# The last two down rounds of each feed-forward, one token half after the other

## The reference, cut to what matters

```python
D_MODEL, SEQ, DEPTH, D_FF = 1024, 512, 2, 2816
def swiglu(h, w_in, w_out):
    g, u = jnp.split(h @ w_in, 2, axis=-1)
    return (jax.nn.silu(g) * u) @ w_out
# per layer i, m = nine modulation vectors from silu(c) @ w_mod[i] + b_mod[i]
h = h + 0.5 * m[2] * swiglu(modulate(rms_norm(h), m[0], m[1]), w_ff_in[i, 0], w_ff_out[i, 0])
a = modulate(rms_norm(h), m[3], m[4])
h = h + m[5] * mixer(a)          # Fourier mixing (i = 0) or convolution (i = 1)
h = h + 0.5 * m[8] * swiglu(modulate(rms_norm(h), m[6], m[7]), w_ff_in[i, 1], w_ff_out[i, 1])
```

## Time and profile before

| | us |
|---|---|
| median of 3 runs | 1851.25 (1850.66 to 1855.26) |
| span of the profiled execution | 1854.0 |
| TensorE busy in it | 1803.4 (97%) |
| VectorE busy in it | 1198.1 (65%) |
| ScalarE busy in it | 619.6 (33%) |
| mean granted TensorE clock | 0.989 |

### The profile page before, as it was taken

The page is one execution under the profiler, slowest core; times in us unless marked ns, Lnnn a source line. Parts: engine busy times, 40 slices in busy tenths (PEclk is TensorE's granted clock), DMA queues, the critical chain, the costliest instruction groups (busy, mean ns, idle before and its releaser), DMA issues.

```text
span 1854.0 us, 22066 instructions
## 1 busy us (share of the span) xinstructions
PE 1803.4 (97%) x8604; PEld 1486.5 (80%) x8604; DVE 1198.1 (65%) x1541; ACT 619.6 (33%) x796; POOL 171.7 (9%) x148
## 2 busy tenths in 40 slices
PE   5899999998999999999999999999999999999999
PEld 2688888888898888888988888889764898888888
DVE  5876767667867676666676766547798555444454
ACT  2522222234342223222432222225776542222221
POOL 0000000002110000000200000002995200000000
PEclk8999999998999999999999999999999999999999
DMA  7753634431436354363154353411120321313201
GB/s 279 273 201 114 212 127 155 185 113 47 136 114 227 114 176 164 122 218 114 69 196 145 140 200 113 136 68 46 46 91 25 116 88 69 136 68 113 90 23 69
DMA packets 160395, 238.10 MB, mean 128 GB/s; under 512 B 3805, under 2 KB 110509, under 8 KB 160204
## 3 DMA queue, kind: packets, MB, share of 16 engines
q1 hardware_dynamic: 160016, 236.99, 36.5%
q10 hardware_dynamic: 316, 0.23, 0.0%
HBM read 235.11 MB, written 2.10 MB: 128 GB/s over the span
## 4 chain that ended last, share of the span: by engine, by line
PE 84%; DVE 6%; POOL 4%; ACT 3%; DMA 1%; issue 1%; SPq 0%; POOLq 0%; DVEq 0%; ACTq 0%
PE bank L1670 15%; PE bank L1672 15%; PE bank L1677 15%; PE bank L1545 10%; PE bank L1547 10%; PE bank L1546 10%; POOL tmp_c L628 3%; DVE mod_acc L1025 2%; PE bank L1927 1%; DVE w_lo L992 1%; PE bank L1617 1%; PE bank L1615 1%; PE bank L1619 1%; DMA raw_pair<-in_w_mod 1%; POOL sq_sum L593 1%
## 5 line engine op out<-in xcount | busy, mean ns | idle before, releaser
L1670 PE MATMUL bank<-a_hi,w_hi 128*128 128x512 f32 x1408 | 551.9, 392 | 6.2 <-ACT a_hi L686 4.7
L1672 PE MATMUL bank<-a_hi,w_lo 128*128 128x512 f32 x1408 | 548.9, 390 | 0.0
L1677 PE MATMUL bank<-a_lo,w_hi 128*128 128x512 f32 x1408 | 434.5, 390 | 1.3 <-DVE a_lo L1100 1.2
L1670 PEld LDWEIGHTS bank<-a_hi,w_hi 128*128 128x128 f32 x1408 | 265.0, 188 | 63.4 <-issue 6.3
L1218 DVE SCALAR_TENSOR_TENSOR h<-bank,half_gate,h 128x512 f32<-128x512 f32 x320 | 233.3, 745 | 121.7 <-PE bank L1547 121.1
L1677 PEld LDWEIGHTS bank<-a_lo,w_hi 128*128 128x128 f32 x1408 | 264.6, 188 | 57.3 <-DVE a_lo L1100 2.3
L1672 PEld LDWEIGHTS bank<-a_hi,w_lo 128*128 128x128 f32 x1408 | 264.9, 188 | 56.2 <-issue 1.4
L1545 PE MATMUL bank<-p_hi,w_hi 128*128 128x512 f32 (+1 forms) x768 | 289.5, 377 | 1.5 <-DVE h L1225 0.9
L1547 PE MATMUL bank<-p_lo,w_hi 128*128 128x512 f32 (+1 forms) x768 | 287.5, 374 | 0.0
L1546 PE MATMUL bank<-p_hi,w_lo 128*128 128x512 f32 (+1 forms) x768 | 287.4, 374 | 0.0
L992 DVE TENSOR_TENSOR w_lo<-raw_pair,w_hi 128x2048 fp32r<-128x2048 f32 x102 | 235.4, 2308 | 51.8 <-ACT w_hi L800 47.9
(11 more groups left out here) (197 smaller groups left out, 1849.2 us busy)
## 6 DMA issues: line engine op xcount, KB each, us to landing
raw_pair<-in_w_ff_in SPq DMA_DIRECT2D x88, 1024.0 KB, 7.0
raw_mod<-in_w_mod SPq DMA_DIRECT2D x66, 1024.0 KB, 8.4
raw_down<-in_w_ff_out SPq DMA_DIRECT2D x44, 1024.0 KB, 8.6
raw_pair<-in_conv_w_in SPq DMA_DIRECT2D x8, 1024.0 KB, 6.8
raw_pair<-in_w_mod SPq DMA_DIRECT2D x6, 1024.0 KB, 16.0
raw_pair<-in_fnet_w_out SPq DMA_DIRECT2D x4, 1024.0 KB, 6.1
raw_pair<-in_conv_w_out SPq DMA_DIRECT2D x4, 1024.0 KB, 6.7
raw_mod<-in_x SPq DMA_DIRECT2D x4, 512.0 KB, 5.6
```

Of the source, the lines that this page charges most:

```text
L1670: pe.matmul(ps[banks + s][:], tile_hi, a_hi[:, k], start=k == 0, stop=False, skip_group_check=True)
L1672: pe.matmul(ps[banks + s][:], tile_lo, a_hi[:, k], start=False, stop=False, skip_group_check=True)
L1677: ins = pe.matmul(ps[banks + s][:], w_hi[b][:, s * KD + k], a_lo[:, k], start=False, stop=k == KD - 1, skip_group_check=True)
```

## The change

Down round 9 is no longer done in the last step. Rounds 9 and 10 are done together after it, first for token half 0 and then for half 1. Both rounds of a chunk and half add up in one PSUM bank, and h is updated once for the two. Six banks (4, 5, 6, 7, 0, 1) are used in turn; since only six chunks fit, a half goes: round 9 d 0 to 5, round 10 d 0 and 1, round 9 d 6 and 7, round 10 d 2 to 7. Before the seventh chunk of round 9 TensorE waits for the update of the first. TensorE waits for `mod_row` of the last unit before the first of these products, in place of before the fourth chunk (d = 3) of the round. In the norm behind it, VectorE's `mod_columns` now stands ahead of the updates of half 0, the second weight unit is split later (ScalarE waits until round 9 has been read in both halves), VectorE's order is another, and `first_two` waits for the second unit only where it is first read. The transposes at the end of the kernel go through banks 2, 3, 0, 1, six of eight ahead of the last down chunk.

```diff
+    LAST_BANKS = [4, 5, 6, 7, 0, 1]
+    LAST_ROUNDS = [(NI - 2, range(6)), (NI - 1, range(2)), (NI - 2, range(6, KD)), (NI - 1, range(2, KD))]
     def last_round_h(f):
-        return HB[FF_PHASE[f]] + KD * (NI - 1)
+        return HB[FF_PHASE[f]] + KD * (NI - 2)
+        def last_bank(hf, d):
+            return ps[LAST_BANKS[(KD * hf + d) % len(LAST_BANKS)]][:, HALF[hf]]
...
 # ScalarE, ff_norm
-                act.wait_ge(s_take, last_round_h(f))
-                next_hi_unit()
                 for o in range(KD):
                     half_square(n, 0, o)
-                for o in range(3):
+                half_std(n, 0)
+                half_hi(n, 0, 0, layer, v)
+                half_hi(n, 0, 1, layer, v)
+                half_square(n, 1, 0)
+                act.wait_ge(s_down_read, f + 1)
+                next_hi_unit()
+                half_square(n, 1, 1)
+                half_hi(n, 0, 2, layer, v)
...
 # VectorE, ff_norm
+                mod_columns(call)
                 for d in range(KD):
                     flush_half(f, 0, d)
-                    if d == 3:
-                        next_lo_unit(0)
-                    if d == 6:
-                        next_lo_unit(1)
-                mod_columns(call)
-                for d in range(3):
-                    flush_half(f, 1, d)
                 half_rstd(n, 0)
-                flush_half(f, 1, 3)
-                for k in range(4):
+                for k in range(2):
                     half_normed(n, 0, k, layer, v)
-                    flush_half(f, 1, 4 + k)
+                    flush_half(f, 1, k)
+                for k in range(2):
+                    half_lo(n, 0, k, layer, v)
+                for k in range(2, 4):
+                    half_normed(n, 0, k, layer, v)
+                    flush_half(f, 1, k)
+                next_lo_unit(0)
+                flush_half(f, 1, 4)
+                next_lo_unit(1)
+                for k in range(2, 4):
+                    half_lo(n, 0, k, layer, v)
+                    flush_half(f, 1, 3 + k)
+                flush_half(f, 1, 7)
...
 # VectorE, ff_step
-                for d in range(KD):
-                    flush(f, i - 1, d)
                 if not last_step:
+                    for d in range(KD):
+                        flush(f, i - 1, d)
                     next_lo(f, i, 1, par)
...
 # TensorE
-                for b, use in units:
-                    pe.wait_ge(s_w[b], use + 1)
+                pe.wait_ge(s_w[units[0][0]], units[0][1] + 1)
...
-                    down(f, i - 1, 1 - par, unit)
+                    if not isinstance(i, int) or i < NI - 1:
+                        down(f, i - 1, 1 - par, unit)
+                    return unit
...
+                if unit is not None:
+                    pe.wait_ge(s_mod_row, unit + 1)
+            def last_down(f, r, hf, ds):
+                hs, final = HALF[hf], r == NI - 1
+                b, use = (DOWN_LAST[f][0], DOWN_LAST[f][1] + 1) if final else (DOWN[f][0], r + DOWN[f][1] + 1)
+                pe.wait_ge(s_w[b], use)
+                pe.wait_ge(s_p, 2 * NI * f + 2 * r + 2)
                 for d in ds:
+                    q, turn = KD * hf + d, len(LAST_BANKS)
+                    if not final and q < 4:
+                        pe.wait_ge(s_h, last_round_h(f) - 3 + d)
+                    elif not final and q < turn:
+                        pe.wait_ge(s_prod, 2 * NI * (f + 1) - 1)
+                    elif not final:
+                        pe.wait_ge(s_h, last_round_h(f) + q - turn + 1)
                     for j in range(2):
+                        ins = product(last_bank(hf, d), w_hi[b][:, j * KD + d], w_lo[b][:, j * KD + d],
+                                      p_hi[:, r % 2, j, hs], p_lo[:, r % 2, j, hs], not final and j == 0,
+                                      final and j == 1)
+                    if final:
+                        ins.then_inc(s_take, 1)
+                    elif q == 2 * KD - 1:
+                        ins.then_inc(s_down_read, 1)
+            def last_rounds(f, n):
+                for part, (r, ds) in enumerate(LAST_ROUNDS):
+                    last_down(f, r, 0, ds)
+                    if part == 1:
+                        mod_transpose(2 if f == 0 else 3 + f)
+                last_down(f, NI - 2, 1, range(3))
                 half_sums(n, 0)
+                last_down(f, NI - 2, 1, range(3, 6))
                 half_spread(n, 0)
+                for r, ds in LAST_ROUNDS[1:]:
+                    last_down(f, r, 1, ds)
+                pe.wait_ge(s_h, last_round_h(f) + KD + 4)
...
 # end of the kernel: OUT_BANK = [2, 3, 2, 3, 2, 3, 0, 1]
+            for r, ds in LAST_ROUNDS:
+                last_down(3, r, 0, ds)
+            last_down(3, NI - 2, 1, range(6))
+            out_transpose(0)
+            out_transpose(1)
+            last_down(3, NI - 1, 1, range(2))
+            last_down(3, NI - 2, 1, range(6, KD))
+            out_transpose(2)
+            out_transpose(3)
+            last_down(3, NI - 1, 1, range(2, 6))
+            out_transpose(4)
+            last_down(3, NI - 1, 1, range(6, 7))
+            out_transpose(5)
+            last_down(3, NI - 1, 1, range(7, KD))
+            out_transpose(6)
+            out_transpose(7)
```

More of the change, by code:

```diff
@@ L128, in hybrid_backbone @@
     PROJ = [(o, None) for o in range(KD - 2)] + [(o, hf) for hf in range(2) for o in (KD - 2, KD - 1)]
-    for prev, nxt, updates in ((FFA, FNET, KD * (NI + 1)), (FNET, FFB, len(PROJ)), (FFB, FFC, KD * (NI + 1)),
-                               (FFC, CONV, KD * (NI + 1)), (CONV, FFD, len(PROJ))):
+    for prev, nxt, updates in ((FFA, FNET, KD * NI), (FNET, FFB, len(PROJ)), (FFB, FFC, KD * NI),
+                               (FFC, CONV, KD * NI), (CONV, FFD, len(PROJ))):
         HB[nxt] = HB[prev] + updates
@@ L1224, in flush_half @@
                 dve.wait_ge(s_take, last_round_h(f) + KD * hf + d + 1)
[L1225 removed]
+                dve.scalar_tensor_tensor(out=h[:, d, hs], in0=last_bank(hf, d), scalar=half_gate[:, f, d:d + 1],
                                          in1=h[:, d, hs], op0=ALU.mult, op1=ALU.add).then_inc(s_h, 1)
@@ L1633, in first_two @@
                             for b, s, bank in tiles[:3]:
+                                if k == 0 and b == units[1][0]:
+                                    pe.wait_ge(s_w[b], units[1][1] + 1)
                                 half_product(b, s, bank, k, hs, False)
@@ L1761, in last_round @@
-            def last_round(f, n):
-                last_down(f, 0, range(4))
-                mod_transpose(2 if f == 0 else 3 + f)
-                last_down(f, 0, range(4, KD))
-                last_down(f, 1, range(4))
+                    unit = step(i, i % 2, f < 3 and i <= UNIT_STEPS[f])
+                if unit is not None:
[5 more added lines that the diff above has]
+                pe.wait_ge(s_p, 2 * NI * f + 2 * r + 2)
+                for d in ds:
+                    q, turn = KD * hf + d, len(LAST_BANKS)
[5 more added lines that the diff above has]
+                        pe.wait_ge(s_h, last_round_h(f) + q - turn + 1)
+                    for j in range(2):
+                        ins = product(last_bank(hf, d), w_hi[b][:, j * KD + d], w_lo[b][:, j * KD + d],
[5 more added lines that the diff above has]
+                        ins.then_inc(s_down_read, 1)
```

53 lines of the change are left out of this document (15 added, 38 removed).

## The result

The change makes the kernel slower. Its median is 1863.53 us of 4 runs (1862.91 to 1865.42) beside 1852.53 us of 4 runs of the kernel before (1850.66 to 1855.26): a ratio of 1.006 with a 95% interval of 1.0048 to 1.0073, +11.0 us by the medians. The forecast was 1860.5 us in a range of 1855.0 to 1865.0, slower by more than 0.3% with a chance of 0.76. The range holds the time; the forecast's own range, 1858 to 1863, does not, and the sum was 3.0 us short.

A forecast was written before the change was run, and what follows sets the result against it. TensorE, busy 97% of 1854.0 us, was taken as the bound. Ending terms of +4.4, +3.4, +0.2 and +1.3 made +9.3 us, added to 1851.25 (the span less 2.75): 1860.5 us, range 1855.0 to 1865.0.

The forecast's parts named there:

- The wait for `mod_row`: Ahead of the first down product in f = 0 and 1, TensorE waits 3.15 us each; before, this cost nothing.
- The clock behind it: After the `mod_row` wait, one half-rate stretch of 3.4 us, 1.6 us lost, in each of f = 0 and 1.
- The sign on the norm's stretches: The forecast is wrong if the norm's slow clock stretches, worth 6.2 us before, vanish.
- Rival A: Neither the idle 3.1 us nor the sums draw a half-rate stretch: +6.1 us, or +5 (1856.3); chance 0.20.
- Rival B: More or longer half-rate stretches behind the idle time or norm sums, +1.5 us each, 1864 with two or three; chance 0.20.
- Rival C: First wait under 1 us, clock up throughout: -0.2 us, or about -3 to -6 (1847); chance 0.05.
- Rival D: The Fourier stage's start hides part of f = 0's cost, leaving only 2 us: 1858; chance 0.55 together with the forecast.
- The later loads: SyncE loads the next weight pair some 12 us later, but it is needed over 40 us on: no cost.
- Half products and f = 3: Half products +0.6 us an ending; f = 3's last product 2 us later, tail 0.7 us shorter: +1.3 us.
- The squares of half 0: In the norm, TensorE waits 0.7 us for GpSimd's adds of 1.08 us each; 0.97 us before.
- The second weight unit: Split later, with VectorE parts of 1.6 us, it makes TensorE wait 1.15 us at the next stage.
- The sums of half 1: The sums behind three k of the next stage wait 0.4 us for GpSimd's last add.

The follow-up runs named there:

- e0: The changed kernel run once more with no edit, timed beside the kernel before: 1864.10 us, ratio 1.0067.
- e5: The kernel before with the new ending in f = 2 alone: 1854.41 us against 1850.81, ratio 1.0017.
- e2: The changed kernel with the sums that `mod_row` reads in bank 1 and the wait only at the sixth chunk: 1854.57 us, ratio 1.0013.
- e10: The kernel before with only the early wait for `mod_row`, ahead of round 9's first chunk in f = 0 and 1: 1862.71 us, ratio 1.0058.
- e4: The kernel before with the new ending in f = 3 alone: 1853.94 us against 1850.81, ratio 1.0014.
- e3: The kernel before with only down round 9 done in half products of 256 tokens: 1854.40 us against 1851.15, ratio 1.001.
- e1: The changed kernel with the wait for `mod_row` moved back to the fourth chunk of round 9: 1856.55 us, ratio 1.0027.
- e9: e11 with the second weight unit ahead of the Fourier mixing split only behind the norm of half 1: 1845.82 us, ratio 0.9967 to the kernel before.
- e7: e2 with the old ending in f = 3 and two half 0 updates ahead of `mod_columns`: 1852.34 us, ratio 1.0 to the kernel before.
- e11: e7 with half 1's square sums behind k = 3 in place of k = 2: 1849.10 us, ratio 0.9984 to the kernel before.
- e8: The changed kernel with twelve unneeded 128x512 products ahead of the wait for `mod_row`: 1862.67 us, ratio 1.006 to the kernel before.

## Why the forecast was right, and where it was short

**The sum, term by term, beside the profile of before.** For f = 0 to 3 the forecast was +4.4, +3.4, +0.2 and +1.3, +9.3 in all. Stages *a* to *d* moved by +4.6, +3.0, -0.4 and +1.9 in e0, 9.1 us, and by +1.1, +2.9, +2.9 and +1.9 in after, 8.8 us. So e0 has every term within 0.6 us, and after has two of them 3 us off, in opposite directions, by its clock.

**The same without the clock.** Stages that have no half-rate stretch in them give this directly. *b* is 47.9 us with the old ending (e5) and 48.2 with the new one and no wait (e2): +0.3. *c* is 257.8 (e10) and 258.1 (e0): +0.3. *d* is +1.8 (e4). For *a* no such pair is there; e2's 141.0 lies between e3's 140.4 and before's 142.6, so the new ending costs about nothing there. The two waits are 6.3 us. Together some 8.7 us, so at medians of +11.0 and +13.0 the clock costs some 2 to 4 us.

The forecast has it the other way round. It took two new stretches, +3.2 us, and the old ones as gone, -(1.6 + 3.05 + 1.6) = -6.25 us: 3.05 us given back, and 12.35 us for work and waits. By that price f = 1 is 3.4 - 1.6 + 3.05 = 4.85 against 3.45 measured, f = 2 0.2 + 1.6 = 1.8 against 0.3. The old stretches were priced too high, at 0.47 of their length: they cost 50.0 - 47.9 = 2.1 us in f = 1 and 0.7 in f = 2. So the work and the waits were some 3.7 us too dear and the clock 5 to 7 us too cheap, and the two leave a sum only 3.0 us short of the median. That part of the hit is luck.

**The wait for `mod_row`, right.** Forecast 3.15 us in f = 0 and 1, measured 2.98 + the semaphore, in both. e2 and e10 take it out and put it in by itself and get 9.5 and 10.7 to 11.8 us. It is the larger part of the result.

**The clock behind it, right on the mean and not in its place.** Forecast was one stretch of 3.4 us behind each wait. After had none in f = 0 and one in f = 1; e0 had more than one in f = 0 (401.00 to 411.00 at a mean of 0.66) and one in f = 1. Over the two waits e2 gives 3.2 us, as forecast, e10 4.4 to 5.5. The wrong idea in it was that a stretch belongs to its wait: after and e0 are the same kernel, with the same waits, and have their stretches in different places. A clock of 1.00 behind the wait was one of the forecast's signs of being wrong, and f = 0 of after has it. The sign on the norm's stretches contradicts the sum, which takes all of them as gone: those behind the squares of half 0 did go, others came behind half 1.

**Rival A, the clock holds,** is refused: e1 and e2 gave back more than the idle time. **Rival B** came nearer than the sum. It had 1864 us for more stretches, and the medians are 1863.53 and 1864.10. Stretches came behind the sums of half 1 (437.90 and 1281), and e0 had one of 6.8 us behind the first wait; those behind the old ending's squares went. Beside the one profile of before there is no more slow clock (mean 0.991 after, 0.990 in e0, 0.989 before). Beside the runs there is: of the 75 runs of the kernel before that stand beside the experiments, 43 have a mean clock of 0.991 to 0.993, median 0.992; the 9 of the change have 0.988 to 0.991, median 0.990. Its second reason is not borne out. The rule of the Trainium skill (TensorE: Matmul & The Clock Gate, "A second HAM failure mode: psum-queue depth-cycling") has the clock swing while banks are cycled with short pauses between. Here the 32 half chunks through six banks in f = 3, with 0.5 us of idle time in all, and the 26.90 us of f = 2, with one of 0.78 us, ran at 1.00. In the endings and the norms the slow stretches came behind waits of 0.9 us or more, and not behind all of them. **Rival C** is refused by 2.98 us: it needed a first wait under 1 us. **Rival D** holds in part: without the clock f = 0 cost some 3.15 us and not 4.4. The later loads cost nothing, as forecast: the stretches from the first to the last gate product are as long as before.

**Half products and f = 3.** The last product of f = 3 was forecast 26.1 us after the start; it ends at 1855.11 + 0.28 = 1855.39, 26.15 us behind 1829.24. The tail behind it was forecast at 2.8 us and is 1858.68 - 1855.39 = 3.3: the last pair of transposes waits 0.58 us for the update, and three copies still follow in turn behind the one at 1855.83. Together +1.8 (e4, stage *d*) in place of +1.3.

**The squares of half 0: mis-sized.** Forecast a wait of 0.7 us from adds of 1.08 us each; it is nil, since they took 0.85. The trace has the reason: the two long ones before ran beside VectorE's weight parts, and none of these does now. **The second weight unit: mis-sized.** Forecast a wait of 1.15 us, from parts of 1.6; they took 1.23 and 1.37, and the wait is 0.16. (Before, the second part took 1.46.) **The sums of half 1: mis-sized the other way,** 1.09 us for 0.4. The three together were 2.25 in the sum and are 1.25.

**f = 2: a step that failed by its clock.** The sum gave +0.2 us, because it set the half-rate stretch of before (1.6 us) against the new waits and took it as gone. In e0 it is gone, and *c* is -0.4. In after a stretch is there again, from 1281, behind the wait at the half 1 sums, and *c* is +2.9; e5 gives +2.7. In both, 1.7 us of this are the second stretch, in the convolution, 130 us behind the ending (e2, with that one alone, has 259.8). There TensorE idles for 2.3 us in every profile. None of the four profiles with the old ending of f = 2 (before, e3, e4, e10) has a stretch there, and seven of the eight with the new one have one there (all but e0). Whether the new ending brings it was not tried.

**f = 0.** The forecast gave it +4.4. Stage *a* went up by 1.1 in after and by 4.6 in e0, and 3.15 is the wait. What moves it up and down is the clock, of which the profile of before had more than the forecast had looked at: its clock at the start of the Fourier mixing, outside the window of the earlier trace rows, is the second of these lines.

```profile
423.00:431.00 8.00, 6.96 (x42) 6.55 (x42) 3.96 (x12) 3.39 (x10) 3.82 (x7) 0.79 0.80 263
434.00:447.00 13.00, 9.97 (x53) 9.35 (x52) 9.09 (x25) 6.29 (x18) 0.01 (x1) 0.61 0.01 2
885.00:905.00 20.00, 18.85 (x126) 18.25 (x127) 15.49 (x36) 9.80 (x25) 9.95 (x12) 0.83 0.46 159
```

**The time it was set against, the step that failed.** The sum was +9.3 us on the profiled execution, a span of 1863.3; it is 1861.1. Stages *a* to *d* grew by 8.8 us, near the sum, and the start, which has nothing to do with the change, was 1.4 us shorter. Against the medians the sum was 1860.5, and they are 1863.53 and 1864.10. The reason is that the profile of before is of an execution at the slow end of its runs. In the profiles that followed, a run's time is 1.8 us above its span (1862.91 and 1861.1 in after, 1851.78 and 1850.0 in e3), so 1854.0 belongs to some 1855.8, not to a median of 1851. The old endings, all but the half products, are in e3 too, with the same windows:

```profile
423.00:431.00 8.00, 5.46 (x41) 4.99 (x42) 5.36 (x14) 4.43 (x12) 4.55 (x7) 1.00 0.77 257
434.00:447.00 13.00, 10.85 (x72) 10.47 (x73) 10.29 (x27) 6.63 (x18) 0.00 (x0) 0.75 0.00 1
885.00:905.00 20.00, 18.88 (x140) 18.34 (x141) 13.98 (x35) 8.70 (x22) 8.21 (x11) 0.91 0.46 159
```

There the clock is 1.00 where before has 0.79, 0.75 where it has 0.61, and 0.91 where it has 0.83: each time some 3.4 us less at the half rate. Its start is 70.7 us, where before has 72.3. The forecast took the 2.75 us between span and median for a constant, and counted as there to be given back slow clock that more than half of the runs of the kernel before do not have.

**What stays open.** What decides whether a wait of 1 us draws a half-rate stretch in one execution and not in the next was not found. e9 leaves the kernel with two places that still do, at the Fourier mixing (425.00 to 445.00 at 0.74) and in the convolution. Nor was the gain of e7's order of the first two updates measured apart from the rest, nor e9's Fourier edit without e11's.

## What to carry to other kernels

When a group of products is moved ahead of the point where a small reader's bank was wanted, look first at who still reads a bank of the new set: one misplaced wait in front of a nearly idle-free engine cost more than the rest of the change, and giving the small sum another bank (e2) returned 9.5 us. Hide a wait behind work that is needed anyway (e11, one k later); filling it with work that is not needed (e8) brought back nothing that the times can show. Do not book a half-rate stretch to one wait from one profile: it stood elsewhere in the next execution of the same kernel. Before a difference is worked out against one profile, place that profile among the kernel's runs by its own time.

## What the runs showed of the hardware

- The granted clock's half-rate stretches in the stages *a* to *c* were 3.4, 6.8, 10.2 or 13.7 us long, such as 874.20 to 877.60. They began between 0.9 us ahead of the end of a wait (e10, at 876.2, the wait ends at 877.16) and 2.5 us behind it (after, at 1280.5, the wait ends at 1278.02). The waits were of 0.9 to 3.3 us, and only some executions had a stretch at a given wait.
- A half-rate stretch of 3.4 us cost 1.7 us in the convolution (*c* of e2 and e0) and 0.7 us in the old ending of f = 2 (*c* of before and e10).
- An idle wait of 3.15 us cost 4.7 to 5.9 us (e2: 9.5 for two; e10: 10.7 to 11.8 for two).
- 12 products put into the wait kept the clock at 1.00 behind it, but e8's profile was at the half rate for 20.5 us in *a* to *d*, as long as e0's without them.
- GpSimd's add of 128x256 took 0.74 us, and 1.09 to 1.53 us in the adds named above that ran beside a part of VectorE's weight split. VectorE's low part of 128x1024 took 1.23 to 1.37 us in the new order and 1.46 to 1.65 before.
